# Moving the last outputs behind the first channel weights, and three other changes of order, in an fp32 block kernel on one core

## The reference

```python
i_in, z_f, z_b, q_in, gate_a, u_f, gate_f = split_proj(h @ w_in)
o_f, s_f = chunk_scan(q, k_f, v, g_f, s0_f)            # states from a prefix of 256 tokens
o_b, s_b = chunk_scan(flip(q), flip(k_b), flip(v), flip(g_b), s0_b)
o = rmsnorm_of_heads(o_f + flip(o_b)) * hn_w
y_a = o * silu(gate_a)
spec = fftn(u_f in groups, axes=(sequence, channel)).real
y_f = (spec @ w_fourier[group] + b_four) * silu(gate_f)
x = x + gate * (concat([y_a, y_f]) @ w_out)
out = rmsnorm(x, final_norm_w)
```

## Time and profile before

| | |
|---|---|
| median of 3 runs | 2205.48 us (2204.68 to 2206.7) |
| the profiled execution's own time | 2205.83 us |
| its span, first to last instruction | 2204.1 us |
| mean granted TensorE clock | 0.988 |
| PE busy | 2114.9 us, 96% |
| DVE busy | 1531.6 us, 69% |
| ACT busy | 508.3 us, 23% |
| heads, from the span's start | about 515 to 1684 us |
| Fourier part | about 1684 to 1837 us |

### The profile page before, as it was taken

The page is one execution under the profiler, slowest core; times in us unless marked ns, Lnnn a source line. Parts: engine busy times, 40 slices in busy tenths (PEclk is TensorE's granted clock), DMA queues, the critical chain, the costliest instruction groups (busy, mean ns, idle before and its releaser), DMA issues.

```text
span 2204.1 us, 48217 instructions
## 1 busy us (share of the span) xinstructions
PE 2114.9 (96%) x20564; PEld 1776.8 (81%) x20564; DVE 1531.6 (69%) x3275; ACT 508.3 (23%) x836; POOL 75.0 (3%) x109
## 2 busy tenths in 40 slices
PE   5899999999999999999999999999996999999997
PEld 3799988788788788888887887877776887888886
DVE  5865854026777878787787778798896886555554
ACT  3711133111112111212121122111112343212121
POOL 0001101000000000000000000000000010000000
PEclk9999999999999999999999999999997999999999
DMA  8444555342424333333334243333335366534451
GB/s 316 159 131 144 183 156 155 120 132 74 130 83 132 106 115 100 117 111 98 117 94 135 83 132 96 110 112 116 103 103 193 139 229 231 196 127 162 149 177 57
DMA packets 229863, 298.89 MB, mean 136 GB/s; under 512 B 14934, under 2 KB 159990, under 8 KB 226322
## 3 DMA queue, kind: packets, MB, share of 16 engines
q1 hardware_dynamic: 145346, 178.38, 25.1%
q10 hardware_dynamic: 73952, 81.18, 10.8%
q0 software_dynamic: 10352, 36.25, 5.1%
HBM read 198.16 MB, written 97.59 MB: 134 GB/s over the span
## 4 chain that ended last, share of the span: by engine, by line
PE 88%; DVE 5%; DMA 2%; issue 1%; ACT 1%; SPq 1%; ACTq 0%; POOL 0%; DVEq 0%
PE all_bank L61 25%; PE all_bank L63 23%; PE all_bank L62 23%; PE all_bank L1479 3%; PE all_bank L1469 2%; PE all_bank L1423 2%; PE all_bank L1439 2%; PE all_bank L1452 1%; PE all_bank L1462 1%; PE all_bank L1478 1%; DVE hidden_h_lo L483 1%; DMA front_w_mod<-in_w_ada 1%; SPq L366 1%; PE all_bank L1008 1%; PE all_bank L2566 1%
## 5 line engine op out<-in xcount | busy, mean ns | idle before, releaser
L61 PE MATMUL all_bank<-hidden_h_hi,head_hi 128*128 128x512 f32 x1184 | 491.0, 415 | 2.2 <-issue 2.2
L63 PE MATMUL all_bank<-hidden_h_hi,head_lo 128*128 128x512 f32 x1184 | 465.4, 393 | 0.0
L62 PE MATMUL all_bank<-hidden_h_lo,head_hi 128*128 128x512 f32 x1184 | 463.1, 391 | 0.0
L1515 ACT ACTIVATE head_projected<-all_bank 128x512 f32<-128x512 f32 x148 | 88.6, 599 | 864.2 <-PE all_bank L63 864.2
L63 PEld LDWEIGHTS all_bank<-hidden_h_hi,head_lo 128*128 128x128 f32 x1184 | 222.6, 188 | 51.8
L61 PEld LDWEIGHTS all_bank<-hidden_h_hi,head_hi 128*128 128x128 f32 x1184 | 222.9, 188 | 47.4 <-issue 2.5
L62 PEld LDWEIGHTS all_bank<-hidden_h_lo,head_hi 128*128 128x128 f32 x1184 | 223.4, 189 | 41.7 <-issue 2.0
L1615 DVE RECIPROCAL head_inverse<-head_gate 128x448 f32<-128x448 f32 x64 | 185.8, 2930 | 0.0
L1666 DVE TENSOR_TENSOR head_query<-head_query,head_total 128x256 f32<-128x256 f32 x256 | 107.8, 421 | 81.9 <-PE all_bank L1439 51.4
L61 PE MATMUL all_bank<-front_hi,hidden_h_hi 128*128 128x256 f32 x512 | 143.8, 281 | 0.0
L63 PE MATMUL all_bank<-front_hi,hidden_h_lo 128*128 128x256 f32 x512 | 142.7, 279 | 0.0
(11 more groups left out here) (294 smaller groups left out, 4151.4 us busy)
## 6 DMA issues: line engine op xcount, KB each, us to landing
head_raw<-in_w_in POOLq DMA_DIRECT2D x37, 512.0 KB, 4.8
head_value<-value_rows SPq DMA_DIRECT2D x64, 256.0 KB, 5.2
head_query<-piece_query SPq DMA_DIRECT2D x64, 256.0 KB, 6.7
head_out<-head_o ACTq DMA_DIRECT2D x64, 256.0 KB, 6.1
tail_o<-head_out SPq DMA_DIRECT2D x32, 512.0 KB, 5.9
front_raw<-in_w_in SPq DMA_DIRECT2D x19, 512.0 KB, 5.1
front_stage<-in_x SPq DMA_DIRECT2D x16, 512.0 KB, 6.9
front_w_mod<-in_w_ada SPq DMA_DIRECT2D x8, 1024.0 KB, 13.6
```

The source lines that it names most:

```text
L61: nc.tensor.matmul(out, st_hi, mv_hi, start=start, stop=False)
L62: nc.tensor.matmul(out, st_hi, mv_lo, start=False, stop=False)
L63: return nc.tensor.matmul(out, st_lo, mv_hi, start=False, stop=stop)
L1515: nc.scalar.activation(projected[unit % 2][:], ps_proj[unit % 2][:], PIECES[name][1], scale=PIECES[name][2]).then_inc(proj_copied, 1)
```

## The change

Four edits of order, without new work:

1. `outputs`, `rows_out` and `chain` become functions that `heads` hands over. For the last step (head 7, group 3) they are called from the tail: PE's outputs behind `channel_weights(0)`, DVE's chain behind the clearing of `mid_st`, `u` and `mid_w`, ACT's output copies and stores behind the first fold and both channel weights, whose order changes too. The load of `hn` moves from ACT's first place to behind the second fold.
2. ACT's wait for `o_stored` moves from ahead of the middle row to ahead of part f = 4 of the first group; ahead of f = 2 there is a wait for the stores of the projected pieces.
3. `split_due` knows a level 5, behind the DVE loop, for slots over 6 (they were level 4, between the two reciprocals).
4. `load_f(2)` comes ahead of `load_o(0)` on SP, and `split_f_low(2)` ahead of `add_directions(0)` on DVE.

```diff
@@ heads, PE step @@
             project_half(h, g, 9)
-            for d in range(2):
-                wait_count(pe, copied[d], MASKED * n + MASKED)
-                wait_count(pe, chained[d], CHAIN * n + TPG)
-                ... the outputs' matmuls
+            if not (last and g == NG - 1):
+                outputs(pe, h, g)
@@ heads, ACT step @@
+            if not (last and g == NG - 1):
+                rows_out(act, h, g)
@@ heads, DVE @@
-                if (step, max(1, min(slot - 2, 4))) == (g, level):
+                if (step, max(1, 5 if slot > 6 else min(slot - 2, 4))) == (g, level):
...
                 if not ends:
                     prepare(*next_step(h, g), 2 * i + 1)
+            due = split_due(h, g, 5)
+            if due is not None:
+                split_low(h, due)
...
-            for j in range(TPG):
-                ... the chain's instructions
+            if not ends:
+                chain(v, h, g)
@@ tail, SP @@
+        load_f(2)
         load_o(0)
-        load_f(2)
@@ tail, DVE @@
         nc.vector.memset(mid_w[:].bitcast(F32), 0.0).then_inc(mid_w_cleared, 1)
+        left.chain(v, HEADS - 1, NG - 1)
         v.wait_ge(set_once, 2)
         fold_again(0, 0)
         fold_again(0, 1)
+        split_cw_low(0, 0)
         split_fold_low(0, 0)
-        split_cw_low(0, 0)
...
+        split_f_low(2)
         add_directions(0)
-        split_f_low(2)
@@ tail, ACT @@
-        act.dma_start(hn[:], hgrn_cols_in).then_inc(hn_here, DMA)
         act.wait_ge(left.proj_done, left.all_units)
-        split_fold_high(0, 0)
         split_cw_high(0, 0)
-        split_fold_high(0, 1)
+        split_fold_high(0, 0)
         split_cw_high(0, 1)
+        left.rows_out(act, HEADS - 1, NG - 1)
+        split_fold_high(0, 1)
+        act.dma_start(hn[:], hgrn_cols_in).then_inc(hn_here, DMA)
         split_fold_high(0, 2)
...
-        for d in range(2):
-            act.wait_ge(left.o_stored[d], left.steps * DMA)
...
             for f in range(8):
+                if n == 0 and f == 2:
+                    for sem in left.proj_stored:
+                        act.wait_ge(sem, left.all_units // 2 * DMA)
+                if n == 0 and f == 4:
+                    for d in range(2):
+                        act.wait_ge(left.o_stored[d], left.steps * DMA)
@@ tail, PE @@
         channel_weights(0)
+        left.outputs(pe, HEADS - 1, NG - 1)
         for n in range(FG):
             middle(n)
```

More of the change, by code:

```diff
@@ L1173 @@
     steps: int
+    outputs: object
+    rows_out: object
+    chain: object
 def heads(nc, block, r, front_room, work, spare, bank, handed, w_in, one_minus_lb, ident, masks, h_hi, h_lo, states, value_rows, scratch, o_rows):
@@ L1296, in next_step, with tile, outputs, rows_out @@
         return (h, g + 1) if g < NG - 1 else (h + 1, 0)
+    def tile(ap, t):
+        return ap[:, t * P:(t + 1) * P]
+    def outputs(pe, h, g):
+        n, b = NG * h + g, g % 2
+        for d in range(2):
+            wait_count(pe, copied[d], MASKED * n + MASKED)
+            wait_count(pe, chained[d], CHAIN * n + TPG)
+            for t in range(TPG):
+                before = t if d == 0 else TPG - 1 - t
+                if g >= NG // 2:
+                    nc.tensor.matmul(ps[d][2][:, t, :], score[group_of(d, g)][:, t, :], value[d][b][:, t, :], start=True, stop=False)
+                done = nc.tensor.matmul(ps[d][2][:, t, :], tile(query[d][b], t), state[d][:, before, :], start=g < NG // 2, stop=True)
+            done.then_inc(product[d], 1)
+    def rows_out(act, h, g):
+        n = NG * h + g
+        for d in range(2):
+            wait_count(act, product[d], PROD * n + OUT)
+            wait_count(act, o_stored[d], n * DMA)
+            if n == 0:
+                for sem in handed.stored:
+                    act.wait_ge(sem, handed.all_stored)
+            nc.scalar.activation(o[d][:], ps[d][2][:], ACT.Copy).then_inc(o_copied[d], 1)
+        for d in range(2):
+            wait_count(act, o_copied[d], n + 1)
+            t = group_of(d, g) * GRP
+            act.dma_start(o_rows[d][t:t + GRP, bass.ds(h * P, P)].rearrange("(t p) n -> p t n", p=P),
+                          o[d][:]).then_inc(o_stored[d], DMA)
+    def chain(v, h, g):
+        n = NG * h + g
+        for j in range(TPG):
+            for d in range(2):
+                t = j if d == 0 else TPG - 1 - j
+                wait_count(v, chained[d], CHAIN * n + j + 1)
+                if j == 0:
+                    wait_count(v, product[d], PROD * n + INC)
+                    wait_count(v, totalled[d], TOT * n + TOT)
+                nc.vector.scalar_tensor_tensor(state[d][:, j + 1, :], state[d][:, j, :], total_of(d, P)[:, j:j + 1],
+                                               ps[d][1][:, t, :], ALU.mult, ALU.add).then_inc(chained[d], 1)
     @block.gpsimd
@@ L1723, in heads @@
                    o_copied=o_copied, o_stored=o_stored, w_here=w_here, all_products=PROD * NG * HEADS,
-                   all_units=FIRST_UNIT[HEADS], units_of_head=FIRST_UNIT[1], steps=NG * HEADS)
+                   all_units=FIRST_UNIT[HEADS], units_of_head=FIRST_UNIT[1], steps=NG * HEADS,
+                   outputs=outputs, rows_out=rows_out, chain=chain)
 HALF, QUART = SEQ // 2, SEQ // 4
```

28 lines of the change are left out of this document (3 added, 25 removed).

## The result

The changed kernel takes 2188.58 us (2188.04 to 2189.41, 4 runs) against 2206.09 us (2204.68 to 2206.73) on the same chip: a ratio of 0.992, 95% interval 0.9906 to 0.9934. The profiled execution has a span of 2187.0 us against 2204.1.

The account below looks back on a forecast made before the run. PE, busy 96% of the span, was taken to bound the kernel, so only its stops and half clock could give time. Terms -5.8 - 2.4 - 2.5 = -10.7 us gave 2194.8 from the median, stated as 2195.0; range 2190 to 2200.

Parts of the forecast that it names:

- Part 1: Late split in heads 0 to 5: PE's six 0.97 us waits for DVE's state chain go; 5.8 us faster.
- Part 2: Passage from the heads' last increments to the tail's last wave group: reordered work, stores landing at 1702.6; 2.4 us faster.
- early landing: Passage: head stores get through before loads start, or get over one record a turn; 2187 to 2190.5 us, 12%.
- The prediction's paragraph on the Trainium skill: Passage: if queues took turns by packets, the stores would land well before 1694.9, giving 10.3 us; trace said to disagree.
- Part 3: Tail, third Fourier columns first: PE's 2.81 us stop goes, a later 2.1 us wait appears; 2.5 us faster.
- if that new gap drops the clock: Tail, third columns: lower bound of 0.9 us gain, if PE's new wait brings another 3.2 us of half clock.

Follow-up runs that it names:

- the waits alone: The kernel before with only ACT's waits for the head stores moved to the third and the fifth part; ratio 0.9993 (0.9979 to 1.0007).
- the split alone: The kernel before with only the late split, level 5 of `split_due`; ratio 0.9961 (0.995 to 0.9973).
- the third columns alone: The kernel before with only the third Fourier columns loaded and split first; ratio 0.9987 (0.9972 to 1.0002).
- the passage alone: The changed kernel with the late split and the third columns put back as before; ratio 0.9965 (0.9953 to 0.9978).
- The run with the wait back: The changed kernel with ACT's waits for the head stores back ahead of the middle row; ratio 0.9946 (0.9931 to 0.996).

## Why the prediction was wrong, point by point

**Part 1 was right, slightly too small.** Reason, place and what remains of DVE's idle time came as worked out. The term was 6 x 0.97 = 5.8. The eight traces with the new split have 1126.8 us of heads in the mean (1122.9 to 1131.4), the six with the old one 1133.2 (1131.1 to 1135.0): 6.4 us. PE's waits for the state chain are 5.7 or 5.8 us in each of the six, and gone in each of the eight. The spread of the stretch has another source, which was not found: the waits put down to "issue" vary only between 6.5 and 9.8 us.

**Part 2 failed in one step: the landing.** The prediction had the stores' "first records come at 1689.7 (3.6 us after issue, as today by the queue's windows)", then sharing one for one with 4 MB of loads, and landing 16.5 us after issue. Measured: first records a microsecond after issue, both landed by 8.7 us. I took the 3.6 us as a property of the store, and it was one of the queues. In five traces SP issued the first two tables, of 512 KB each, 0.8 and 0.4 us ahead of the first store, and the third, of 1 MB, behind it. In three of them (the kernel before twice, and the waits alone) the third came 0.1 us behind the first store and ahead of the second; no store record moved for 3.4 us, and the landings were 15.5, 15.7 and 15.7. In the other two (the split alone, the third columns alone) it came 0.7 us behind the first store and behind the second as well; the first store record moved after 1.8 us, and the landings were 13.9 and 8.7. Where the queue had run empty, 1059 records moved in the first 3 us, 987 of the stores' 1024 among them. Why a store behind loads moves nothing at all for 3.4 us, though the queues take turns later, no run shows. The rival "early landing" named this mechanism and gave 2187 to 2190.5, at 12%. The evidence for weighing it higher stood in my own text: SP's tables start at 1679.3 and are through by 1686.5, the stores are issued at 1686.1, the fourth table follows at 1687.5. Only the 3.6 us put the stores behind it.

The prediction's paragraph on the Trainium skill was worked out wrongly. It gave the stores a packet a turn and the loads one record; with packets on both sides the shares stay one for one, that case would not have given 10.3 us, and the equal counts of the earlier trace rows speak for neither.

All else of the part held: ACT's arrival at the fifth part (17.6 against 18.3 us), no gap in front of the channel weights, and the work from the fifth part to the last table split (6.3 us against 6.6). With the landing at 8.7 us instead of 16.5, the prediction's own sum gives 7.8 us more than 2.4, that is 10.2; measured 10.05.

**A part of it was the base.** My term was made against one trace, with 35.2 us. The same code gave 28.9 to 36.0 in four traces. Against the mean the passage gains 7.6 us, and the run with the passage alone gained 7.7 (0.35% of 2204.69). The measured times vary likewise, 2197.9 to 2212.0 us for the kernel before in 25 runs, and 2188.8 to 2192.7 for the changed one in four beside them.

**Part 3 was right in its steps and wrong in its choice between bounds.** PE waits 2.41 us for `a_lo` (predicted 2.1), and the operand is ready 0.4 us earlier than before (predicted 0.7). I took 2.5 us as the value, and 0.9 "if that new gap drops the clock". It did: 0.50 from 1839 to 1842. The single-part run gave 0.96, the changed kernel 0.31, and all seven traces with the edit against the six without it 0.4 (151.0 against 151.4). As the six alone lie between 150.6 and 152.2, none of these figures is clear of no gain at all; the bound would have been the nearer term. I should have taken it, since the stop of 2.81 in the old trace was followed by just this.

**Sum.** -7.0 - 10.05 - 0.3 make 17.3 on a difference of the spans of 17.1; the first increments come 0.2 us later. In the means over all traces it is 6.4 + 7.6 + 0.4 = 14.4; the two measurements gave 17.5 (2206.09 - 2188.58) and 15.3 (2206.19 - 2190.94).

What stays open: why two of four traces of the old passage were shorter is known by half. In those SP's issue of the second table took 1.09 and 1.14 us and not 0.43, which put the third behind both stores:

```profile
1679.14 1.09 SPq L1955 DMA_DIRECT2D tail_tab_raw<-in_tables  x1
```

What made that issue slow was not tried. Nor is it known why the changed kernel, with the same issues 1.1 us apart, sometimes has some store records left when the fourth table's begin to move, and sometimes none; the last section shows what such a rest costs.

## What to carry to other kernels

When a wait ends at a transfer's landing, list which queue is issued first around it and by how much, and price both orders: here two stores of 256 KB landed in 3 us alone, in 3 to 9 with a microsecond's lead over the loads, and in 9 to 16 behind the first megabyte of them. Treat a latency read in one trace as made by the transfers around it, and profile the kernel before twice when a term rests on a meeting of two queues. When PE's stop is filled, take the next stop's clock from the last one like it: a stop of 2.4 us brought as much half clock as one of 2.8.

## What was unexpected of the hardware

- In the first trace of the changed kernel the second store of 256 KB landed 8.7 us behind its issue (1679.90), although all but 37 of the stores' 1024 records had moved in the first 3 us. From 1683.3 to 1688.6 queue 10 moved 29 records beside 293 of the load queue. 18 of the 29 are store data, most of them 0.33 us apart, which is one load record of 8 KB (309 ns) and one store record (27 ns); the last starts at 1688.06. So some twenty records that were left when the loads came took turns with them, one for one, and made the landing nearly 6 us later. In the second trace none was left, and the store landed after 2.9 us. The run with the wait back had 55 left at the same point, and its landing came at 9.3. The Trainium skill (DMA: Bandwidth & Descriptors, Queues, rings and completion order) says that a semaphore's increment lands only behind all earlier writes of its DMA engine, those of other queues too. This trace neither needs that rule nor speaks against it, as data moved until half a microsecond before the landing.

```profile
q1 hardware_dynamic: 293, 2.14, 100.1%
q10 hardware_dynamic: 29, 0.01, 0.7%
```

- A stop of 1.13 us ahead of the middle product was followed by half clock in the second trace of the changed kernel (granted clock 0.67 from 1683.8 to 1687.8, and 0.50 within it from 1685.8) and not in the first (1.00 from 1680 to 1688). Of the seven traces in which this stop was 1.13 or 1.14 us, four had half clock behind it and three had not. The two passages differ by 0.4 us only: in the first ACT waited 1.27 us for the landing, in the second 0.8 us for PE.

```profile
1683.80:1687.80 4.00, 4.00 (x24) 3.79 (x23) 3.71 (x8) 2.79 (x8) 0.00 (x0) 0.67 1.02 326
```
